# Two transformer blocks on one core: stages joined into one block, and ACT's copies of the filter transforms moved in its order

## The reference, cut to what matters

```python
# first block
n = rmsnorm(x, norm1_g)
proj = n @ w_in                       # gated linear attention, and dilated attention
o = concat([gla(proj), dilated_attention(proj)])
h = x + o @ w_out
x = rmsnorm(h + hier_moe(rmsnorm(h, norm2_g)), final_norm_g)      # 32 experts, two a token
# second block
h = rmsnorm_2(x, g_mix)
a_x, a_gate, hy, gates = split(h @ w_in_2)
y_a = (rg_lru(conv(a_x)) forward + backward) * gelu(a_gate) @ w_a_out
filt = hyena_filters(...)             # a small network's output @ w3, times a decay
y_b = (two long convolutions of hy with filt, by FFT) @ w_b_out
x = x + (sigmoid(gates) mix of y_a, y_b) @ w_o
out = rmsnorm_2(x + experts_by_choice(rmsnorm_2(x)))              # 16 experts
```

## Time and profile before

| what | value |
|---|---|
| median of three runs | 4154.72 us (4151.86 to 4156.81) |
| profiled execution, its own time | 4151.45 us |
| its span, first to last instruction | 4149.8 us |
| PE, DVE, ACT, POOL busy | 3842.5 us (93%), 2861.6 (69%), 1836.7 (44%), 302.0 (7%) |
| mean granted clock of PE | 0.967 |

### The profile page before, as it was taken

How to read it: one execution, slowest core, us unless ns; L and a number is a source line. 1 busy time by engine, 2 the same in 40 slices (tenths; PEclk the granted TensorE clock), 3 DMA queues, 4 the chain that set the end, 5 groups by cost and what they waited for, 6 DMA issues and landing times. The chain is left out here.

```text
span 4149.8 us, 42556 instructions
## 1 busy us (share of the span) xinstructions
PE 3842.5 (93%) x16620; PEld 2929.3 (71%) x16620; DVE 2861.6 (69%) x2700; ACT 1836.7 (44%) x1693; POOL 302.0 (7%) x279
## 2 busy tenths in 40 slices
PE   7979999699999789999999997979599999999998
PEld 3547787488887577777787633567378888888887
DVE  2645345688888574556344589974588888888887
ACT  3143341377777332444011101210077777777776
POOL 0000000101111100000000000000001111101010
PEclk9989999899999899999999998989899999999999
DMA  3002004699999552221325413233489999999998
GB/s 113 1 20 97 19 12 141 237 398 398 399 399 398 202 174 74 70 68 53 122 86 179 142 56 137 76 127 125 174 311 377 375 377 376 375 376 374 376 376 322
DMA packets 422941, 883.01 MB, mean 213 GB/s; under 512 B 22253, under 2 KB 118841, under 8 KB 421660
## 3 DMA queue, kind: packets, MB, share of 16 engines
q1 hardware_dynamic: 382012, 754.61, 50.4%
q0 software_dynamic: 26640, 97.01, 6.7%
q10 hardware_dynamic: 14160, 29.63, 1.9%
HBM read 784.98 MB, written 96.21 MB: 212 GB/s over the span
## 5 line engine op out<-in xcount | busy, mean ns | idle before, releaser
L2046 DVE TENSOR_TENSOR moe_w_rest<-moe_w_w,moe_upper 128x2048 fp32r<-128x2048 f32 x384 | 862.7, 2289 | 160.7 <-ACT moe_upper L1949 83.8
L1949 ACT ACTIVATE moe_upper<-moe_w_w 128x2048 fp32r<-128x2048 f32 x192 | 357.5, 1910 | 238.8 <-PE moe_y_ps L1913 111.5
L2046 DVE TENSOR_TENSOR moe_w_rest<-moe_w_w,moe_upper_w 128x2048 fp32r<-128x2048 f32 x192 | 431.1, 2288 | 16.9 <-ACT moe_upper_w L1967 16.7
L1967 ACT ACTIVATE moe_upper_w<-moe_w_w 128x2048 fp32r<-128x2048 f32 x192 | 357.7, 1910 | 136.6 <-PE moe_up_ps L1887 75.0
L1957 ACT ACTIVATE moe_upper<-moe_w_w 128x2048 fp32r<-128x2048 f32 x192 | 357.4, 1918 | 0.0
L1887 PE MATMUL moe_up_ps<-moe_upper,moe_x_upper 128*128 128x512 f32 x768 | 311.3, 405 | 0.0
L1887 PE MATMUL moe_gate_ps<-moe_upper,moe_x_upper 128*128 128x512 f32 x768 | 305.4, 398 | 4.7 <-DVE moe_x_rest L2059 4.7
L1887 PE MATMUL moe_gate_ps<-moe_w_rest,moe_x_upper 128*128 128x512 f32 x768 | 304.9, 397 | 0.0
L1887 PE MATMUL moe_gate_ps<-moe_upper,moe_x_rest 128*128 128x512 f32 x768 | 304.6, 397 | 0.0
L1913 PE MATMUL moe_y_ps<-moe_upper_w,moe_hidT_upper 128*128 128x512 f32 x760 | 302.2, 398 | 2.6 <-DVE moe_hidT_rest L2064 2.1
L1887 PE MATMUL moe_up_ps<-moe_upper,moe_x_rest 128*128 128x512 f32 x768 | 303.8, 396 | 0.0
(11 more groups left out here) (580 smaller groups left out, 7810.6 us busy)
## 6 DMA issues: line engine op xcount, KB each, us to landing
moe_w_w<-in_expert_w_dram SPq DMA_DIRECT2D x96, 2048.0 KB, 16.5
moe_w_w<-in_w_gate_dram SPq DMA_DIRECT2D x64, 2048.0 KB, 10.4
moe_w_w<-in_w_up_dram SPq DMA_DIRECT2D x64, 2048.0 KB, 9.7
moe_w_w<-in_w_down_dram SPq DMA_DIRECT2D x64, 2048.0 KB, 9.5
tmp_y_rows<-moe_y ACTq DMA_DIRECT2D x32, 512.0 KB, 7.1
block_w_first<-in_w_in_dram SPq DMA_DIRECT2D x20, 512.0 KB, 3.9
tmp_h<-out_xn POOLq DMA_DIRECT2D x16, 512.0 KB, 3.3
tmp_spectra<-held_K ACTq DMA_DIRECT2D x8, 1024.0 KB, 5.0
```

The source lines that it names most:

```text
L1949: act.activation(half(upper1(c), h), half(weights.w1[c % 2], h), ACT.Copy).then_inc(m.w1_rounded, 1)
L1967: act.activation(half(upper2(i, c), h), half(weights.w2[c % 2], h), ACT.Copy).then_inc(m.w2_rounded, 1)
L2046: dve.tensor_tensor(half(rest, h), half(whole, h), half(upper, h).bitcast(F32), ALU.subtract).then_inc(done, 1)
```

## The change

Four places.

1. The first normalisation and gla_phase stand in one block. SP issues low, gate, q/k and v weights right behind x (`GlaInputs.load`); PE makes the first low product in four parts behind the turns of t = 4 to 7, when `turned_copied` has reached 4. ACT makes one more Sqrt, on eps, at its start. gla_phase skips that product. The normalisation's squares, and q, k and the sums of gla_phase, use buffers of attention (`AttentionInputs`).
2. The split of wq and of the normalised input moves from attention_phase into the last part of gla_phase: one `round_n` on ACT behind `mix_ready` and one in each tile t, `rest_of_n` on DVE in t = 0, 2, 4, 6 and 7 (the last three stay in attention). SP loads wq once the branch's last product is made. The network's seven loads go from SP's queue to POOL's, ahead of the memset of the zeros, and its first products stand behind g = 1 and not ahead of g = 0.
3. overflow_phase, combine_phase and lru_gates_phase stand in one block. A class `FilterInputs` holds the filters' inputs; SP issues their eight loads at the start of the overflow program, reads n_over, and then raises `over_done`, for which POOL, DVE, ACT and PE wait ahead of their combine programs. ACT's copies of the transforms stand in another place of its order.
4. In lru_gates_phase each half of AX waits for `h_split` to be 4 and 8. Once the filters' last set is made SP loads two weight tiles, AG and GA, into their inputs' place; the other buffers wait for `combined.left`.

```diff
@@ norm_phase, PE, behind the turn of tile t
+            if t >= NT // 2:
+                pe.wait_ge(turned_copied, NT // 2)
+                next_inputs.first_low(pe, transposed, t - NT // 2)
@@ norm_phase, ACT
+        act.activation(rms[:, 0:1], eps[:, :], ACT.Sqrt).then_inc(m.roots_ready, 1)
```

```diff
@@ attention_phase
             @block.gpsimd
             def _(pool):
+                network.load(pool)
                 pool.memset(zeros[:, :], 0.0).then_inc(zeros_ready, 1)
...
                     for g, (n, h) in enumerate(PROJ):
+                        if first(i) and g == 2:
+                            network.products(pe, turned, 0)
...
@@ overflow_phase, SP
+            held.load_weights(sp)
+            held.load_decay(sp, 0)
+            held.load_table(sp)
             where_needed(sp, load, lambda: sp.wait_ge(m.y_stored[0], 16 * N_OVER))
+            sp.sem_inc(over_done, 1)
...
@@ combine_phase, ACT
+            act.wait_ge(over_done, 1)
             act.wait_ge(step, 1)
...
+            held.copy(act, 0)
             root(x[0], 0, 0, added)
             for t in range(NT):
                 b = t % 2
                 if t + 1 < NT:
                     root(x[1 - b], 0, t + 1, added)
                 if t >= 2:
                     held.store(act, t - 2)
                     round_turned(t - 2)
                 act.wait_ge(n1_ready, t + 1)
                 act.dma_start(x2[bass.ts(t, P), :], n1[b][:, :]).then_inc(stored[b], 16)
                 root(n1[b], 1, t, n1_ready)
-                held.copy(act, t)
+                if t + 1 < NT:
+                    held.copy(act, t + 1)
...
@@ wide_product
-def wide_product(nc, out, w, rhs_T, tiles=range(ND)):
+def wide_product(nc, out, w, rhs_T, tiles=range(ND), before_half=None):
     for h in range(2):
+        if before_half:
+            before_half(h)
```

More of the change, by code:

```diff
@@ L157, in norm_phase @@
+def norm_phase(nc, block, m, src, gain, ident, transposed, next_inputs):
     BY_ACT = [t for t in range(NT) if t % 2]
     BY_DVE = [t for t in range(NT) if t not in BY_ACT]
[L159 to L243, removed]
@@ new lines, in _, with square, norm @@
+    @block.vector
+    def _(dve):
+        dve.memset(eps[:, :], EPS).then_inc(eps_set, 1)
+        def square(t):
+            dve.wait_ge(x_loaded[t], 16)
+            dve.tensor_tensor_reduce(out=squares[BY_DVE.index(t) % 2][:, :], in0=xt[t][:, :], in1=xt[t][:, :], scale=1.0, scalar=0.0, op0=ALU.mult, op1=ALU.add,
+                                     accum_out=ssum[:, t:t + 1]).then_inc(summed_dve, 1)
+        def norm(t):
+            dve.wait_ge(rms_ready, t + 1)
+            dve.reciprocal(rstd[:, t:t + 1], rms[:, t:t + 1]).then_inc(rstd_ready, 1)
+            dve.wait_ge(rstd_ready, t + 1)
+            dve.scalar_tensor_tensor(xn[t][:, :], xt[t][:, :], rstd[:, t:t + 1], gain_b[:, :], ALU.mult, ALU.mult).then_inc(xn_ready, 1)
+        square(0)
+        for t in range(NT):
+            if t + 1 in BY_DVE:
+                square(t + 1)
+            if t == 0:
+                dve.wait_ge(gain_loaded, 16)
+            norm(t)
@@ L844 @@
+                for hd in range(GLA_H):
+                    cols = bass.ts(hd, GLA_V)
+                    last = dve.scalar_tensor_tensor(o_n[t % 2][:, cols], bank[t % 2][:, cols], rstd[:, t, hd:hd + 1], gate[:, t, cols], ALU.mult, ALU.mult)
+                last.then_inc(on_ready, 1)
 DILATIONS = ((128, 1), (512, 4), (2048, 16))
@@ L1031, in _ @@
             def _(act):
-                for k in range(ND):
-                    act.activation(n_parts.upper[:, k, :], n_parts.whole[:, k, :], ACT.Copy).then_inc(n_rounded, 1)
                 def pair(i):
@@ new lines, in _ @@
+        @block.sync
+        def _(sp):
+            for t in range(NT):
+                b = t % 2
+                if t >= 2:
+                    sp.wait_ge(n1_ready, t - 1)
+                sp.dma_start(x[b][:, :], x1[bass.ts(t, P), :]).then_inc(x_loaded[b], 16)
+                if t == 0:
+                    for j, gain in enumerate((gain1, gain2)):
+                        sp.dma_start(g[j][:, :], row(gain).partition_broadcast(P)).then_inc(g_loaded, 16)
+                elif t == NT // 2:
+                    held.load_second_decay(sp)
+                    ahead.load(sp, next_w)
@@ new lines, in _, with turn @@
+        @block.tensor
+        def _(pe):
+            def turn(t):
+                pe.wait_ge(n2_ready, t + 1)
+                if t >= 2:
+                    pe.wait_ge(h_split, t - 1)
+                turn_rows(nc, n2[t % 2], turned[t % 2], ident).then_inc(n2_turned, 1)
+            pe.wait_ge(over_done, 1)
+            for t in range(NT):
+                if t % HF == 0:
+                    held.make_filters(pe, t // HF)
+                held.transform(pe, t)
+                if t:
+                    turn(t - 1)
+            turn(NT - 1)
```

1678 lines of the change are left out of this document (892 added, 786 removed).

## The result

The changed kernel takes 4177.98 us (median of four runs, 4177.43 to 4178.94), the kernel before 4153.29 in four runs of the same comparison: 1.0059 of it, with a 95% interval of 1.0043 to 1.0075. It is slower by 25 us, 0.6%. 4176 was forecast, with a range of 4150 to 4196. The profiled execution of the changed kernel has a span of 4177.3 us.

What follows compares the result with a forecast made beforehand. PE was taken to work nearly throughout, so time lost in a block shifts all behind it. -10.2 - 12.0 + 0 - 7.0 + 11.7 + 30.8 + 8.1 - 5.6 + 6.6 = +22.4; forecast 4176 us, range 4150 to 4196.

Steps and rivals of the forecast that it cites:

- The first rival: Combine stage: new order costs nothing per pair, periods stay at 33.5 us; 4119 to 4122 us in all; chance 0.12.
- the milder chain: Combine stage: stores land in time and the clock falls only at AX; +10 us, 4162 to 4165; chance 0.12.
- The stall on the store: Odd transforms from T(3): the copy waits for the store of u-3 to land; a stall of 3.6 us.
- The clock: PE below full speed after three pauses of 12 to 14 us and one in AX: 4 x 1.65 = +6.6 us.
- T(0) and T(1): First two transforms of the combine stage: T(0)'s earlier copies let T(1) end sooner, -7.0 us.
- T(2): Third transform: starts 22.4 us after T(1)'s end, before 10.5 to 10.7, as DVE's decay comes later; +11.7 us.
- the two periods: T(2) to T(4) and T(4) to T(6): 48.8 to 48.9 us each against 33.5; +30.8 us.
- the end: Last part of the combine stage, from T(6): 31.7 us against 23.6; +8.1 us.
- the recurrent stage: After turn(7): AX's first half starts at once, AG starts 15.7 us after turn(7), before 21.2; -5.6 us.
- First block: Normalisation and recurrent branch: earlier table load, first low product behind the last four turns; -10.2 us.
- Attention: Attention's inputs: splits moved earlier, k product starts 12.0 us sooner; at 1.94 us per POOL issue 4.1 of it go.
- Start of the stage: Combine stage's start: filters at 1404.9 rather than 1402.27, but the table decides the first transform either way; 0 us.

Runs made afterwards that it cites:

- the last run: The changed kernel with the first low product's 16 records behind all eight turns of the first normalisation, not between the last four: 4176.82 us, one run.

## Why the prediction was right, and where not

**The order of ACT's copies decides.** Right in mechanism, place and sign, and shown by three kernels: the order alone costs 53 us, taken back it gives 55, and with DVE's decay moved T(2) follows T(1) as before. What the order had to win in a steady period was small from the start. Before, PE waited 0.88 us for ACT's copies there:

```profile
1474.71 7.17 PE L3494 MATMUL held_fwd_ps<-held_filt,held_tr 128*128 128x256 f32 x32 [0.88 <-ACT held_K L3506]
```

Now it waits 2.85. The stations were measured where they were forecast: 13.7 us to the decay, with 13.5 worked out. The first rival (the chain costs nothing) and the milder chain fall.

**The stall on the store.** Forecast 3.6, measured 2.85; ACT waited 1.8 us of it for the landing. Right in kind; the run with the store issued first moved it by 1.65.

**The clock** was mis-sized: +6.6, and it came to about +15.7. I had one slow stretch of 1.65 behind each pause. There were two: the 24 filter records behind the pause (2.4, 2.0 and 1.9 over 5.82) and the second half of the odd transforms behind the stall of 2.8 us (1.7 each, three times); T(1) had 2.65 (before it had 1.6, which the forecast counted as won back), and AX's second half 1.74 (its first half was as slow, but ended ahead of the wait). Together 6.3 + 5.1 + 2.65 + 1.74 = 15.7.

**The steps without the clock.** With these 15.7 taken off where they arose, T(0) and T(1) give -6.9 (forecast -7.0), T(2) +11.2 (+11.7), the two periods +28.6 (+30.8), the end +7.1 (+8.1) and the recurrent stage -5.6 (-5.6). The lengthenings were a little too long, by 3.7 in all, and the clock 9.1 too short. (The terms listed for a period add up to 49.4 and not to the 48.8 to 48.9 that were used; without the clock it measured 47.8. With 49.4 the sum would have been 1 us higher.) In all, to AG the profiled pair has +29.3 for +22.4. The medians differ by only 24.7, as the pair loses 1.8 again behind AG, most of it by a slow stretch of the kernel before, and that kernel scatters by 6 us over its runs. That 4176 was met to 2 us is in part luck.

**First block.** Forecast -10.2, measured -9.2. The 1 us is again the clock, 1.9 us in the gate's product. The second low product ended at 37.3 as forecast, but that the parts between the turns save 6.9 us, as the expectation of the last run had it, was wrong: without them the turns end 3.2 us sooner, the low products 1.9 us later, and the q and k products start at the same time.

**Attention.** -12.0 forecast, -11.9 measured. POOL's loads end at 295.4 in the profile after, the k split at 302.2, 4 us before it is wanted. The bound by 1.94 us an issue did not come about: the seven issues took 0.57 to 0.73 us each, six of them beside DVE's three differences. Nor did the one from the Trainium skill ("SBUF — State Buffer", "SBUF: two separate sides"). That page's rule is for certain operations of DVE, its example a copy; the differences here are TENSOR_TENSOR operations, so this trace neither bears the rule out nor contradicts it. No run takes the moved splits back, so that the 12 us are theirs is read from the order of the operations.

**Start of the stage.** The filters start 18.7 us behind the experts' last product, before 15.4, so 3.3 us late where 2.6 had been forecast, and T(0) did not move. But what decides T(0) is no longer the table: its row names DVE's filters as what it waited for last.

**Recurrent stage.** AG starts 17.3 us behind turn(7), with 15.7 forecast and 1.74 of clock in the second half of AX.

## What to carry to other kernels

When an engine serves two chains from one queue, moving its work for the one chain ahead puts it ahead of the other's: here the copies that free PE's banks came at once, and the roots on which DVE's next 13 us depend came behind PE's longest product. Before moving an operation, write down for each engine what waits behind it and who waits for that, through one whole period; a wait of PE of 0.88 us in a steady period was not worth 18 us on the period. An idle time on PE can also cost clock: look for a slow stretch behind every wait, not behind one a period, and give it a range, since behind equal waits of 2.3 and 2.8 us it came in some places and not in others.

## What the runs showed of the hardware

- PE waited 2.8 us in the odd transforms and the 32 records behind took 8.86 instead of 7.17 us; after a wait of 1.2 (store first) or 0.88 they took 7.17. With 2.8 to 2.9 it happened in all three places of the changed kernel, but in one of three in the kernel with the order alone and in one of three in each of the two where PE was kept busy. Behind a wait of 2.30 us eight other records took 5.37 us before and 3.67 after. What tells these apart stays open.
- In the first block the granted clock fell to 0.50 from about 40 us in the changed kernel, from 44.4 with the low product behind the turns, and from 52 before, each time with the same wait of 0.86 us ahead of the gate's product. PE's own waits don't explain these places.
- A store of 1 MB took 11.8 us to land where it ran beside a load of x, two gathers, the load of the decay and that of a weight tile; the median of that run is 4.7.
- POOL's issues of small transfers took 0.57 to 0.73 us, six of the seven beside DVE's differences (TENSOR_TENSOR).
